# Layer 0's modulation columns: 16 ahead of the first norm, 32 on GpSimd and ScalarE beside the attention

## What is computed

```python
cond = jax.nn.silu(c)
for l in range(DEPTH):
    mod = cond @ w_ada[l] + b_ada[l]
    sh1, sc1, ga1, sh2, sc2, ga2 = [m[:, None, :] for m in jnp.split(mod, N_MOD, axis=-1)]
    h = rmsnorm(x, g_norm1[l]) * (1.0 + sc1) + sh1
    z = h @ w_in[l]
    ...   # three mixers: chunked gMLP, sparse attention with a top-256 selection, convolution
    x = x + ga1 * mix
    h2 = rmsnorm(x, g_norm2[l]) * (1.0 + sc2) + sh2
    x = x + ga2 * ((jax.nn.silu(h2 @ w_gate[l]) * (h2 @ w_up[l])) @ w_down[l])
```

## Time and profile before

| what | us |
|---|---|
| median of 3 runs (3189.17 to 3191.08) | 3190.39 |
| the profiled execution's own time | 3190.63 |
| its span, first to last instruction | 3188.9 |
| PE busy | 2901.9 (91%) |
| DVE, ACT, POOL busy | 1513.9, 1001.6, 592.7 |
| first matmul of the input projection starts at | 118.79 |
| attention of layer 0, from first exponential to last reciprocal | 474.6 to 690.9 |

### The profile page before, as it was taken

One profiled execution on the slowest core, in us unless ns is written; L12 is line 12 of the kernel. 1 busy time (PEld: TensorE's weight loads), 2 busy tenths in 40 slices (PEclk: granted clock), 3 DMA queues, 4 the chain that ended last, 5 costly groups with the idle time before them and its releaser, 6 DMA issues.

```text
span 3188.9 us, 42697 instructions
## 1 busy us (share of the span) xinstructions
PE 2901.9 (91%) x16242; PEld 2531.2 (79%) x16266; DVE 1513.9 (47%) x2504; ACT 1001.6 (31%) x1228; POOL 592.7 (19%) x254
## 2 busy tenths in 40 slices
PE   6699868899799999999979987889979999999996
PEld 6678753349799999999968876333879999999996
DVE  7656776633443242333454678664333323343244
ACT  1335636623411111111143564563341111111113
POOL 0220220001122222222214123000112221322221
PEclk9999979999999999999989998999899999999998
DMA  8313100011122222212232221001112212222222
GB/s 344 116 44 117 41 35 1 1 34 67 53 86 68 77 82 70 96 61 73 80 116 71 88 69 39 1 1 33 56 44 99 69 63 94 64 86 70 81 78 81
DMA packets 71253, 227.00 MB, mean 71 GB/s; under 512 B 16880, under 2 KB 17136, under 8 KB 69744
## 3 DMA queue, kind: packets, MB, share of 16 engines
q1 hardware_dynamic: 68512, 215.16, 20.0%
q10 hardware_dynamic: 2640, 10.49, 0.8%
HBM read 213.54 MB, written 11.54 MB: 71 GB/s over the span
## 4 chain that ended last, share of the span: by engine, by line
PE 72%; DVE 10%; ACT 8%; issue 4%; DVEq 3%; DMA 2%; POOL 1%; ACTq 0%; SPq 0%; POOLq 0%
PE ps L855 59%; ACT notsel L676 5%; PE ps L1082 4%; PE ps L1066 2%; DVE smax L1537 2%; DMA w_ada<-in_w_ada 1%; PE ps L884 1%; DVE w_ada L1213 1%; DVE junk L1213 1%; PE ps L1070 1%; PE ps L1072 1%; DVEq L1320 1%; DVE s_cand L1318 1%; PE ps L1152 1%; PE ps L945 1%
## 5 line engine op out<-in xcount | busy, mean ns | idle before, releaser
L543 POOL TENSOR_TENSOR w_lo<-w_raw,w_hi 128x1024 fp32r<-128x1024 f32 x202 | 496.6, 2459 | 2511.0 <-ACT w_hi L636 2511.0
L855 PE MATMUL ps<-h_hi,w_hi 128*128 128x352 f32 x2928 | 661.6, 335 | 61.4 <-DVE h_lo L1201 47.9
L855 PE MATMUL ps<-h_hi,w_lo 128*128 128x352 f32 x2928 | 637.5, 325 | 0.0
L855 PE MATMUL ps<-h_lo,w_hi 128*128 128x352 f32 x2928 | 636.8, 326 | 0.0
L855 PEld LDWEIGHTS ps<-h_hi,w_hi 128*128 128x128 f32 x2928 | 502.3, 192 | 115.5 <-issue 90.3
L855 PEld LDWEIGHTS ps<-h_hi,w_lo 128*128 128x128 f32 x2928 | 508.2, 190 | 0.0
L855 PEld LDWEIGHTS ps<-h_lo,w_hi 128*128 128x128 f32 x2928 | 504.4, 190 | 0.0
L636 ACT CAST w_hi<-w_raw 128x1024 fp32r<-128x1024 f32 x202 | 211.1, 1045 | 616.9 <-PE ps L855 411.1
L676 ACT ACTIVATE notsel<-score,s_cand 128x384 bf16<-128x384 f32 (+3 forms) x248 | 297.4, 1200 | 142.9 <-DVE s_cand L1318 142.6
L1635 DVE TENSOR_TENSOR act_f<-silu,ps 128x1056 f32<-128x1056 f32 x44 | 55.2, 1254 | 597.8 <-PE ps L855 597.8
L1616 DVE SCALAR_TENSOR_TENSOR x<-ps,mod,x 128x704 f32 (+2 forms) x240 | 125.4, 578 | 397.7 <-PE ps L855 392.0
(11 more groups left out here) (232 smaller groups left out, 3076.7 us busy)
## 6 DMA issues: line engine op xcount, KB each, us to landing
w_ada<-in_w_ada SPq DMA_DIRECT2D x96, 512.0 KB, 4.8
w_raw<-in_w_up SPq DMA_DIRECT2D x88, 512.0 KB, 3.4
w_raw<-in_w_in SPq DMA_DIRECT2D x34, 512.0 KB, 3.6
cw<-in_convw SPq DMA_DIRECT2D x32, 512.0 KB, 4.5
w_ada<-in_w_ada SPq DMA_DIRECT2D x7, 2048.0 KB, 10.3
w_raw<-in_w_down SPq DMA_DIRECT2D x32, 384.0 KB, 3.1
w_ada<-in_w_ada ACTq DMA_DIRECT2D x5, 2048.0 KB, 11.4
w_raw<-in_w_down SPq DMA_DIRECT2D x32, 320.0 KB, 2.9
```

Of the source, the lines that this page charges most:

```text
L543: nc.gpsimd.tensor_tensor(w_lo[slot][:], w_raw[:], w_hi[slot][:].bitcast(F32), ALU.subtract)\
L855: last = nc.tensor.matmul(ps[:, bank + t, 0:TW], wt[slot][:, kk, :], mv[:, kk, t * TW:(t + 1) * TW], start=(kk == 0 and p == 0), stop=(kk ...
```

## The change

Of layer 0's 48 columns, 16 are made ahead of the first norm. 12 of them go to PE the other way round: `cond` with its 2 columns is loaded as weights and 512 columns of the weight move, 8 matmuls for 4 columns of the modulation; ACT copies the 2 x 512 result out of PSUM and PE turns it back with four small matmuls (`turn_ada`). Four go to DVE as before. `rms(0, 0)` and `find_rstd(0, 0)` are put between the second and the third of PE's blocks, and DVE waits for the modulation only after the first `xn`. `modulation` is split in two parts.

The other 32 columns are loaded by SP one by one into three slots in the region of x, ahead of the first `bring_back`. For each, POOL multiplies by both conditioning vectors (two 128 x 1024 instructions), and ACT sums each product (two 128 x 1024 instructions with an accumulator) after the exponential of unit t = 3 + n. POOL waits for ACT to have used column n - 2 before it writes column n; SP waits the same way for a slot. SP's next issues (half of x, the cached keys and values, the output projection's strips) stand behind the last column. The second part of `modulation` runs on DVE ahead of `m_lo`. `cond_row` gets a place of its own and is no longer fetched and put through Silu again in each layer.

```diff
-ADA_PE, ADA_DVE = 5, 7
+ADA_PE, ADA_DVE = 3, 1
+ADA_FIRST = 4 * (ADA_PE + ADA_DVE)
+ADA_SLOTS, ADA_FROM = 3, 3
...
-            for n in range(ADA_DVE):
-                if n >= 2:
-                    sp.wait_ge(ada0_dve.sem, n - 1)
-                m = 4 * (ADA_PE + n)
-                sp.dma_start(w_ada0[n % 2][:], a["w_ada"][DEPTH - 1, m:m + 4].rearrange("m p k -> p m k"))\
-                    .then_inc(ada0_loaded[n % 2].sem, 16)
+            sp.dma_start(w_ada0[0][:], a["w_ada"][DEPTH - 1, 4 * ADA_PE:ADA_FIRST].rearrange("m p k -> p m k")).then_inc(ada0_loaded[0].sem, 16)
...
+                if l == 0:
+                    for m in range(ADA_FIRST, 48):
+                        n = m - ADA_FIRST
+                        if n >= ADA_SLOTS:
+                            sp.wait_ge(later_used.sem, n - ADA_SLOTS + 1)
+                        sp.dma_start(ada_later[n % ADA_SLOTS][:], a["w_ada"][DEPTH - 1, m]).then_inc(later_loaded[n % ADA_SLOTS].sem, 16)
+                    sp.wait_ge(later_used.sem, 48 - ADA_FIRST)
                 for d in range(4):
                     bring_back(d)
...
+                if l == 0:
+                    for n in range(48 - ADA_FIRST):
+                        m = ADA_FIRST + n
+                        pool.wait_ge(later_loaded[n % ADA_SLOTS].sem, (n // ADA_SLOTS + 1) * 16)
+                        w = ada_later[n % ADA_SLOTS]
+                        if n >= 2:
+                            pool.wait_ge(later_used.sem, n - 1)
+                        for c, dst in enumerate((ada_prod[n % 2], w)):
+                            last = nc.gpsimd.tensor_tensor(dst[:], w[:], cond_row[:, c, :], ALU.mult)
+                        last.then_inc(later_times.sem, 1)
...
                     exponentials(t, P, PLACE["S", t], 512)
+                    if l == 0 and 0 <= t - ADA_FROM < 48 - ADA_FIRST:
+                        n = t - ADA_FROM
+                        act.wait_ge(later_times.sem, n + 1)
+                        for c, src in enumerate((ada_prod[n % 2], ada_later[n % ADA_SLOTS])):
+                            last = nc.scalar.activation(src[:], src[:], ACT.Copy, accum_out=mod_raw[:, c, ADA_FIRST + n:ADA_FIRST + n + 1])
+                        last.then_inc(later_used.sem, 1)
...
+            def turn_ada(n):
+
+                pe.wait_ge(ada0_row.sem, n + 1)
+                for e in range(4):
+                    m = 4 * n + e
+                    last = nc.tensor.matmul(ps[:, 7, 2 * m:2 * m + 2], ada_row[n % 2][:, e * P:(e + 1) * P], ident[0:2, 0:2],
+                                            start=True, stop=True)
+                last.then_inc(ada0_turned.sem, 1)
+
             for n in range(ADA_PE):
...
+                for kk in range(KD):
+                    last = nc.tensor.matmul(ps[0:2, n % 2, :], cond[:, kk, :],
+                                            w_ada0[1 + n][:, :, kk * P:(kk + 1) * P],
+                                            start=(kk == 0), stop=(kk == KD - 1))
                 last.then_inc(ada0_pe.sem, 1)
+                if n >= 1:
+                    turn_ada(n - 1)
+                if n == 1:
+                    rms(0, 0)
+            turn_ada(ADA_PE - 1)
...
+                if l == 0:
+                    dve.wait_ge(later_used.sem, 48 - ADA_FIRST)
+                    modulation(l, 1, 2, 6)
```

More of the change, by code:

```diff
@@ L186, in build @@
         Z_O = SC_O + SC_AT[-1] * 4
+        ada_row = [place(f"ada_row{s}", Z_O + s * 2048, [2, 4 * P], F32) for s in range(2)]
         swapped = place("swapped", Z_O, [P, TOK], F32)
@@ L196, in build @@
         recip = place("recip", CS_O + 4096, [64, 2, 512], F32)
-        cond_row = place("cond_row", Z_O, [P, 2, D], F32)
+        ada_later = [place(f"ada_later{s}", o, [P, D], F32)
+                     for s, o in enumerate((X_O, X_O + 4096, X_O + 4 * TILE + 2 * HPW * 4))]
+        ada_prod = [place(f"ada_prod{s}", X_O + 8192 + s * 4096, [P, D], F32) for s in range(2)]
         w_ada = [place(f"w_ada{s}", CS_O + s * 4096, [P, D], F32) for s in range(2)]
@@ L203, in build @@
         sumsq = place("sumsq", H_O + (KD + 7) * TILE, [P, TOK], F32)
-        rstd = place("rstd", R_O + 3 * TILE, [P, TOK], F32)
-        xn = [place(f"xn{s}", R_O + (4 + s) * TILE, [P, TOK], F32) for s in range(2)]
-        hf = [place(f"hf{s}", R_O + (6 + s) * TILE, [P, TOK], F32) for s in range(2)]
+        rstd = place("rstd", R_O + 4 * TILE, [P, TOK], F32)
+        xn = [place(f"xn{s}", R_O + (5 + s) * TILE, [P, TOK], F32) for s in range(2)]
+        hf = [place(f"hf{s}", R_O + (7 + s) * TILE, [P, TOK], F32) for s in range(2)]
         m_hi = place("m_hi", R_O, [P, KD, TOK], F32R)
@@ L601, in square, with find_rstd @@
                 nc.scalar.activation(sq[e][:], x[:, kk, :], ACT.Square).then_inc(sq_ready.sem, 1)
+            def find_rstd(l, which):
+                nc.scalar.preload_act_table_set(LN_EXP)
+                act.wait_ge(rms_summed.sem, rms_summed.at(l, which + 1))
+                power(rstd[:], tiles3(3), -0.5, eps[:, 0:1], 1.0 / D, as3).then_inc(rstd_ready.sem, 1)
             def norm(l, which, final=False):
@@ L644, in _, with ada_row_out @@
             nc.scalar.activation(cond[:], cond_in[:], ACT.Silu).then_inc(cond_ready.sem, 1)
-            for n in range(ADA_PE):
[L646 to L649, removed]
-                if n == 1:
[L651 to L658, removed]
+            def ada_row_out(n):
+                act.wait_ge(ada0_pe.sem, n + 1)
+                if n >= 2:
+                    act.wait_ge(ada0_turned.sem, n - 1)
+                nc.scalar.copy(ada_row[n % 2][:], ps[0:2, n % 2, :]).then_inc(ada0_row.sem, 1)
+            for n in range(ADA_PE):
+                act.dma_start(w_ada0[1 + n][:], a["w_ada0"][4 * n:4 * n + 4].rearrange("m p k -> p m k")).then_inc(ada0_loaded[1 + n].sem, 16)
+            act.wait_ge(consts_made.sem, 1)
+            act.wait_ge(x_loaded.sem, 16)
+            for kk in range(KD):
+                if kk >= 2:
+                    act.wait_ge(sq_taken.sem, kk - 1)
+                square(kk, kk % 2)
+            act.wait_ge(row_loaded.sem, 16)
+            nc.scalar.activation(cond_row[:], cond_row[:], ACT.Silu).then_inc(row_ready.sem, 1)
+            for n in range(ADA_PE):
+                ada_row_out(n)
+                if n == 1:
+                    find_rstd(0, 0)
             for l in range(DEPTH):
@@ L810, in _ @@
                 norm(l, 1)
-                act.wait_ge(row_loaded.sem, row_loaded.at(l, 16))
-                nc.scalar.activation(cond_row[:], cond_row[:], ACT.Silu).then_inc(row_ready.sem, 1)
                 for g, nf in enumerate(GROUPS):
```

91 lines of the change are left out of this document (47 added, 44 removed).

## The result

| kernel | median, us | range | runs | profiled run's own time, span |
|---|---|---|---|---|
| before | 3189.78 | 3188.73 to 3191.08 | 4 | 3190.6, 3188.9 |
| after | 3213.14 | 3210.29 to 3214.59 | 4 | 3212.1, 3210.3 |

The ratio is 1.007, with a 95% interval of 1.0054 to 1.0086: the change makes the kernel slower by 23 us. The forecast was 3226 us, slower, with a range of 3172 to 3254. Both kernels were profiled once; all rows are from these single executions.

A forecast was written before the change was run, and what follows sets the result against it. DVE's column instructions bound the head before the first `hf`, with PE busy 91% of the span. 3190.6 - 56.1 + 6 + 12.6 + 9.6 + 12.9 + 15.1 + 23.9 + 11 gave 3226 us, range 3172 to 3254.

The forecast's parts named there:

- The head: Layer 0 up to the first `hf`: columns moved to PE bring `hf` at 58.6 instead of 114.7 us, -56.1 us.
- Rival (d): Before the first `hf`: PE stays at its lower clock, 20 us more, 3246 us; chance 0.15 shared with rival (c).
- First two columns: Ahead of attention group 2: POOL's multiplications meet `negmax` and the tiny instructions starting the sampled search, +6 us.
- Groups 2 to 5: Layer 0's attention: late last counts plus DVE's waits for POOL, less slack; +12.6, +9.6, +12.9 and +15.1 us.
- Groups 6 and 7: End of layer 0's attention groups: POOL's 12 columns of 4.8 us bound them, 79.7 against 55.8 us, +23.9.
- The fetch: Behind the last column: PE waits 10 us for x, keys and values, plus 1 for going cold; +11, bounds 8 and 16.
- Rival (a): Attention, `select` in groups 2 to 5: DVE's waits hidden or not taken, only ACT's and POOL's pace counts; 3174 us, chance 0.17.
- Rival (b): Attention of layer 0: even ACT's pairs are hidden and only the late fetch shows; 3146 us, chance 0.06.
- Rival (c): Sampled search in the attention: one-element `s_cand` waits for POOL too, 22 us more, 3248; chance 0.15 shared with rival (d).
- the sign "2.4 us above its old length": Profile after, groups 2 to 5: the scan, `negmax` and `s_keep` would each be 2.4 us above their old length.

The follow-up runs named there:

- the run with the head alone: Kernel after with its 16 early columns kept, the 32 later columns neither loaded, multiplied nor summed (sums set to zero); 3133.1 us, ratio 0.982.
- two memset runs: Kernel after with POOL's two multiplications of each later column replaced by five or four 128x1024 memsets; 3187.2 us with five, 3160.2 us with four.

## Why the prediction was right, and where it was off

Against the forecast's sum (3225.6 us, the profiled execution 3212.1) the head won 1.1 us more and the later columns cost 12.4 less. The steps are the ones forecast; most of them were sized too high and one too low, so a small part of the agreement is errors that cancel.

- **The head**, forecast -56.1, measured -57.2. The first block ran at the lower clock level for its first 4 us, as assumed, after PE had done nothing up to there: its first records started 0.85 us apart up to 31.07 us, and 0.43 apart from 31.80 on. The second block's load did not hold PE up; I had it at 38.7 us. That hid the 1.6 us that DVE waited for `w_lo`. Rival (d) is out.
- **First two columns**, forecast +6: the first exponential came 53.1 us earlier (421.51 against 474.63), so +4.1. Two of DVE's instructions waited, `negmax` at 3.32 us (1.23 before) and a `notsel` at 2.90 (0.75). Against the run with the head alone it is 6.8; between the head and this point executions differ by some us.
- **Groups 2 to 5**, forecast +12.6, +9.6, +12.9, +15.1, measured at the first exponential of the next group +10.4, +9.8, +11.0, +12.6. The mechanism is the one forecast, waits of DVE's two-operand instructions one after the other. The term mis-sized is the wait: I charged 2.3 to 2.4 us each; the rows show 1.55 to 2.11. ACT's pair took 2.08 us (453.65 to 455.73 in the rows below), not 2.28.

```profile
453.65 1.05 ACT L820 ACTIVATE ada_prod<-ada_prod 128x1024 f32<-128x1024 f32 x1
454.69 1.04 ACT L820 ACTIVATE ada_later<-ada_later 128x1024 f32<-128x1024 f32 x1
455.73 2.01 ACT L710 ACTIVATE notsel<-score,s_cand 32x2080 bf16<-32x2080 f32 x1
```

- **Groups 6 and 7**, forecast +23.9, measured +21.2: POOL's step was 4.64 us, not 4.8, which is 1.9 of the difference over 12 columns. The last exponentials of group 7 were 4.64 us apart. POOL was busy 116 us more from 400 to 650 us, not 155, because the last nine columns' work lay behind 650.
- **The fetch**, forecast +11 (10 and 1): PE's wait cost 9.9, its slow start 4.0 (four products of 2.08 us where 1.13 was usual; the granted clock from 710 to 730 us was 0.50, the lower level, after PE had stood for 9.8 us). I had priced the wait rightly and the slow start at a quarter. But the kernel before also ran slow a little later (its first products with `q` and `kcache` 2.08 us at 703.00, the granted clock 0.52 from 699 to 708), and 2.0 came back there. Another 2.7 came back up to the end. That is the kernel before's: against the head alone, the kernel after is 78.5 us late at the sampled reciprocal and 78.8 at the end. Moving the fetch gave back 8.9.
- **Rival (a)**, only pace, was forecast at 3174, with DVE's waits not taken. The two memset runs price it: some 3167. The kernel lies 46 us over it, since the waits were taken. Rival (b), only the fetch, was forecast at 3146. Its nearest is the run without multiplications, 3157.5, where the pairs still showed (7.6 us up to the last reciprocal) beside the fetch (11.5).
- **Rival (c)** is out. The one-element `s_cand` starts right beside a multiplication and takes its old 0.21 us:

```profile
578.32 0.21 DVE L1375 TENSOR_SCALAR s_cand<-s_thr,s_bit 128x1 uint32<-128x1 uint32 x1
...
577.89 2.36 POOL L604 TENSOR_TENSOR ada_later<-ada_later,cond_row 128x1024 f32<-128x1024 f32 x1
```

But `s_keep`, one element too and with two operands, did wait where it met a multiplication: 2.22, 2.07 and 1.76 us at 511.37, 556.49 and 607.73, where 0.16 is usual. So one element does not spare an instruction the wait when it has two operands. Elsewhere in groups 2 to 5 `s_keep` was at 0.15 to 0.85, so the sign "2.4 us above its old length" held for a few only.

```profile
511.37 2.22 DVE L1387 TENSOR_TENSOR s_keep<-s_cnt,s_need 128x1 uint32<-128x1 f32 x1
...
511.23 2.34 POOL L604 TENSOR_TENSOR ada_later<-ada_later,cond_row 128x1024 f32<-128x1024 f32 x1
```

On `s_cand`, the Trainium skill says in "SBUF — State Buffer", section "Who interferes with whom", that an instruction of DVE with at most one SBUF input, outside the two-port modes, does not contend; this trace agrees (0.21 us). The same section of the Trainium skill has two-input instructions of DVE contend with GpSimd's reads and not with its writes: the scan at 1.49 us beside memsets and 3.5 to 3.6 beside multiplications agree. By that rule the scan would meet POOL's one-operand form too; the run with it has the scan at 1.49 us, and the measurement decides.

The sum had 91.1 us for the later columns, the trace 83.4 up to the end of PE's slow start and 78.7 at the end of the kernel. Of the 12.4 between, 4.7 came back behind the fetch. The other 7.7 are mostly the waits' size (6.4 in groups 2 to 5, 1.9 ahead of them) and POOL's step (2.7), less the 2.9 by which the fetch was priced too low.

## What to carry to other kernels

An idle engine is not free if its form of instruction reads two operands from SBUF while another engine's critical work does the same: here some 46 of 80 us (an estimate from the two memset runs) were lost where the added multiplications met an engine that the change gave nothing to in that stage. Look first for a gap of the engine that can do the work alone, with the other one idle; 32 columns on the busier VectorE cost 3.4 us, on two idle engines 80. And put no load that waits for a tile ahead of one that the main line needs in the same queue: that alone was 6 to 8 us (5.9 at the eighth gating, 7.6 between the medians).

## What the hardware showed that I had not expected

- POOL multiplying one operand of 128x1024 float32 by a number took 2.77 us, two operands by each other 2.36, a memset 0.95 (1.07 from start to start with a drain between).
- Of these, only the two-operand form stopped DVE's two-operand instructions for about 2 us each; the one-operand form cost them 0 to 0.84 us and waited itself, the memset cost them nothing. `s_keep`, one element and two operands, waited up to 2.1 us for the two-operand form, as long as instructions of 640 and more elements.
- Of DVE's selection, only the one-operand `TENSOR_SCALAR` that makes `notsel` ahead of the scan was held up by memsets: in the kernel with five of them it took 1.23 us in group 2 in place of 0.55.
